# Output projection and first gate/up units of a two-layer decoder step: last squared sums moved ahead, one half-size product moved between two units, other PSUM banks for the last units

## The reference

```python
def rmsnorm(x, g):
    y = x * lax.rsqrt(jnp.mean(x * x, axis=-1, keepdims=True) + EPS)
    return y * g
...
# per layer
m = mixers(rmsnorm(x, g_pre_mix) @ w_in)          # one combined input projection
x = x + rmsnorm(m @ w_out, g_post_mix)            # output projection
h = rmsnorm(x, g_pre_ffn)
x = x + rmsnorm((silu(h @ w_gate) * (h @ w_up)) @ w_down, g_post_ffn)
...
# mixer C: scores of the token indexer
sc = relu(einsum('bthd,bsd->bths', qi, ki))       # 4 index heads
scores = einsum('bth,bths->bts', wi, sc)
```

## Time and profile before

| what | us |
|---|---|
| median of 3 runs | 3017.16 |
| lowest, highest | 3014.57, 3017.43 |
| profiled execution, its own time | 3017.33 |
| its span in the trace | 3015.2 |
| PE busy | 2916.3 (97%) |
| DVE busy | 1783.4 (59%) |
| ACT busy | 1371.4 (45%) |
| POOL busy | 1119.2 (37%) |

### The profile page before, as it was taken

One profiled execution on the slowest core, in us unless ns is written; L12 is line 12 of the kernel. 1 busy time (PEld: TensorE's weight loads), 2 busy tenths in 40 slices (PEclk: granted clock), 3 DMA queues, 4 the chain that ended last, 5 costly groups with the idle time before them and its releaser, 6 DMA issues. The chain is left out here.

```text
span 3015.2 us, 53292 instructions
## 1 busy us (share of the span) xinstructions
PE 2916.3 (97%) x20746; PEld 2541.2 (84%) x20746; DVE 1783.4 (59%) x3508; ACT 1371.4 (45%) x2618; POOL 1119.2 (37%) x846
## 2 busy tenths in 40 slices
PE   8999999999999999999999999998999999999998
PEld 6777756559999999999977777665699999999998
DVE  5579675546865455444555896754578554554551
ACT  4367525555543333444333765354645333334442
POOL 3003031215346656554700110313152555564442
PEclk9999999999999999999999999999999999999999
DMA  5120225553222222667621112356523222236763
GB/s 181 43 65 29 96 89 183 194 187 126 84 76 86 75 82 77 193 183 221 177 71 46 38 46 96 125 174 204 196 63 102 86 65 78 86 98 202 212 195 115
DMA packets 392242, 357.58 MB, mean 119 GB/s; under 512 B 33601, under 2 KB 354010, under 8 KB 391994
## 3 DMA queue, kind: packets, MB, share of 16 engines
q1 hardware_dynamic: 371514, 282.86, 30.9%
q0 software_dynamic: 20480, 71.32, 7.0%
HBM read 299.66 MB, written 54.44 MB: 117 GB/s over the span
## 5 line engine op out<-in xcount | busy, mean ns | idle before, releaser
L750 PE MATMUL ps<-w_in_slots,hT 128*128 128x256 f32 (+1 forms) x2048 | 446.8, 374 | 3.8 <-PEq L214 2.1
L750 PEld LDWEIGHTS ps<-w_in_slots,hT 128*128 128x128 f32 x2048 | 373.0, 192 | 59.1 <-issue 12.8
L2971 POOL TENSOR_TENSOR t_lo<-t_raw,t_hi 128x512 fp32r<-128x512 f32 x190 | 257.0, 1353 | 308.1 <-ACT t_hi L2766 219.0
L2443 PE MATMUL ps<-a_lo,wd_hi 128*128 128x352 f32 x1056 | 345.8, 327 | 5.8 <-DVE a_lo L3120 5.3
L2443 PE MATMUL ps<-a_hi,wd_hi 128*128 128x352 f32 x1056 | 340.5, 322 | 0.0
L2443 PE MATMUL ps<-a_hi,wd_lo 128*128 128x352 f32 x1056 | 340.1, 322 | 0.0
L2994 POOL TENSOR_TENSOR wd_lo<-wd_raw,wd_hi 128x1024 fp32r<-128x1024 f32 x96 | 212.2, 2217 | 210.1 <-ACT wd_hi L2814 209.9
L3086 DVE TENSOR_TENSOR t_raw<-w_pair,w_pair 128x512 f32<-128x512 f32 x120 | 130.6, 1088 | 268.0 <-PE ps L2547 268.0
L2547 PE MATMUL ps<-s_lo,t_hi 128*128 128x264 f32 x960 | 273.4, 285 | 0.0
L2547 PE MATMUL ps<-s_hi,t_lo 128*128 128x264 f32 x960 | 273.2, 285 | 0.0
L2547 PE MATMUL ps<-s_hi,t_hi 128*128 128x264 f32 x960 | 272.8, 284 | 0.0
(11 more groups left out here) (424 smaller groups left out, 7065.2 us busy)
## 6 DMA issues: line engine op xcount, KB each, us to landing
wd_raw<-in_w_down SPq DMA_DIRECT2D x192, 192.0 KB, 3.0
wd_raw<-in_w_down SPq DMA_DIRECT2D x96, 256.0 KB, 3.4
a_in<-apark SPq DMA_DIRECT2D x132, 176.0 KB, 3.9
w_pair<-in_w_gate SPq DMA_DIRECT2D x40, 512.0 KB, 5.2
w_pair<-in_w_up SPq DMA_DIRECT2D x40, 512.0 KB, 5.1
w_in_slots<-in_w_in SPq DMA_DIRECT2D x18, 1024.0 KB, 5.4
apark<-a SPq DMA_DIRECT2D x40, 264.0 KB, 2.1
apark<-t_up SPq DMA_DIRECT2D x40, 264.0 KB, 4.0
```

The lines of the kernel that those rows point to most:

```text
L750: ins = pe.matmul(ps[:m, bank[i], 0:w], hT[:, k, cols(n)], W[:, g % 2, k, 0:w], start=(k == 0), stop=(k == KC - 1))
L2443: ins = pe.matmul(bank(b), w, x, start=first and i == 0, stop=end and i == 2)
L2971: pool.tensor_tensor(t_lo[e][:, :, :], t_raw[e][:, :, :] if len(src) > 1 else src[0], t_hi[e][:, :, :].bitcast(F32), ALU.subtract).then_in ...
```

## The change

1. Input projection: the sample tile `PT` of group CV moves from the last place to between tiles 4 and 5; the chunks of index scores 2 and 3 change places (the 128-column one now comes ahead of the 512-column one). In layer 1 the first `rotate` is issued inside `new_x_left`, at k = 5.
2. Banks: units 7 to 11 use banks 2, 3, 7, 4, 5 where they used 0, 1, 7, 2, 3.
3. PE: `mix_sum_2(0)` one block of three matmuls earlier; `mix_sum_1(2)` behind unit 0 where it was behind unit 1; `mix_sum_2(2)` in the middle of unit 6 where it was behind it; `product(0, 0)` between units 7 and 8 where it was behind unit 11.
4. ACT: `root(2)` before `keep(1, 6)`; `keep(2, 7)` and the rounding of the second weights (`split_w(1)`) ahead of the last three roundings of third 1; the rounding for product (0, 0) behind `root(6)`.
5. POOL: the first rest of the output weights waits for DVE's first rest of the activations.
6. DVE, last third: `sum_comb("s5")` before the wait for POOL's last sum, `sum_weight(0)` behind it, `rest_of_weight(0)` behind `invert(6)`, all ahead of the h loop. `multiply_up(0)` and `(1)` stay behind the h loop.
7. SP: the first `w_pair` loads ahead of the last stores of `xpark`.

```diff
-    units = [... (IX, range(T0, TILES)), (CV, range(T1, TILES))) for n in tiles]
+    units = [... (IX, range(T0, TILES)), (CV, (3, 4, PT, 5, 6, 7))) for n in tiles]
+    chunks[2], chunks[3] = chunks[3], chunks[2]
...
                 for k in range(KC):
+                    if k == 5:
+                        rotate(0)
...
-    unit_bank = lambda n: n if n < 7 else (0, 1, 7, 2, 3)[n - 7]
+    unit_bank = lambda n: n if n < 7 else (2, 3, 7, 4, 5)[n - 7]
...
             for n, (j, th) in enumerate(seq):
+                if n == 8:
+                    product(0, 0)
...
                 for k in range(KC):
+                    if (n, k) == (6, 4):
+                        mix_sum_2(2)
...
-                if n == 1:
+                if n == 0:
                     mix_sum_1(2)
-                if n == 6:
-                    mix_sum_2(2)
             for q in range(NQ):
-                for pos in range(7):
+                for pos in range(0 if q else 1, 7):
...
             keep(1, 5)
+            root(2)
             keep(1, 6)
-            root(2)
...
-            split_h(1, 4, 5, 6, 7)
+            split_h(1, 4)
             keep(2, 7)
+            split_w(1)
+            split_h(1, 5, 6, 7)
...
             root(6)
+            round_weight(0)
             split_h(2, *range(KC))
...
             for k in range(KC):
                 if k:
                     pool.wait_ge(wo_hi_done, k)
+                else:
+                    pool.wait_ge(m_lo, 1)
...
                 if th == 2:
+                    sum_comb("s5")
                     dve.wait_ge(x_add, 3 * (KC - 1))
-                    sum_comb("s5")
+                    sum_weight(0)
                 invert(2 * th + 2)
+                if th == 2:
+                    rest_of_weight(0)
```

More of the change, by code:

```diff
@@ L600, in mix_in @@
     T0, T1 = 5, 3
-    units = [(g, n, 0) for g, tiles in ((IX, range(T0)), (CV, range(T1)), (IX, range(T0, TILES)), (CV, range(T1, TILES))) for n in tiles]
+    units = [(g, n, 0) for g, tiles in ((IX, range(T0)), (CV, range(T1)), (IX, range(T0, TILES)), (CV, (3, 4, PT, 5, 6, 7))) for n in tiles]
     for g in range(CQ, len(blocks)):
@@ L1394, in _ @@
                 g, n, th = units[i]
-                if i in rope_at:
+                if i in rope_at and not (l and i == 0):
                     rotate(i)
@@ L2488, in _ @@
                             pe.wait_ge(m_lo, KC * th + k + 1)
+                        if (th, d, k) == (1, 6, KC - 1):
+                            mix_sum_2(0)
                         if (th, d, k) == (2, 6, 3):
@@ L2741, in silu @@
                 act.activation(sg_first[:, j // 2, of(th)], bank(unit_bank(n)), ACT.Silu).then_inc(sg_done, 1)
[L2743 to L2751, removed]
             def round_comb(n):
@@ L2766, in round_weight @@
                 act.activation(t_hi[e][:, :, :], t_raw[e][:, :, :] if len(src) > 1 else src[0], ACT.Copy).then_inc(t_hi_done, 1)
+            root(5)
+            split_w(2)
+            silu(0)
+            silu(1)
+            split_w(3)
+            square_x(2, *range(KC))
+            root(6)
+            round_weight(0)
+            split_h(2, *range(KC))
             def keep_product(q, pos):
                 act.wait_ge(p_mm, 7 * q + pos + 1)
+                if (q, pos) == (0, 0):
+                    act.wait_ge(mm, len(seq))
                 if q:
@@ L2785, in _ @@
             round_comb("s1")
-            for m in range(3):
+            for m in range(1, 3):
                 round_weight(m)
@@ L3039, in sum_comb, with sum_weight, rest_of_weight @@
                 dve.tensor_tensor(comb_raw[n][:, :, :] if n in s_at else comb_raw[n], x, z, op).then_inc(comb_sum, 1)
+            def sum_weight(m):
+                e, src = m % NT, weight(m)
+                if len(src) == 1:
+                    return
+                dve.wait_ge(w2_in[m // 7 % 2], 32 * (m // 14 + 1))
+                if m >= NT:
+                    dve.wait_ge(p_mm, m - NT + 1)
+                dve.tensor_tensor(t_raw[e][:, :, :], *src).then_inc(t_sum, 1)
+            def rest_of_weight(m):
+                e, src = m % NT, weight(m)
+                dve.wait_ge(t_hi_done, m + 1)
+                dve.tensor_tensor(t_lo[e][:, :, :], t_raw[e][:, :, :] if len(src) > 1 else src[0], t_hi[e][:, :, :].bitcast(F32),
+                                  ALU.subtract).then_inc(t_lo_done, 1)
             dve.wait_ge(g_in, 64)
@@ L3135, in _ @@
             sum_comb("s1")
-            sum_weight(0)
             sum_weight(1)
@@ L3142, in _ @@
             rest_of_comb("s5")
-            rest_of_weight(0)
             dve.wait_ge(mm, 11)
```

53 lines of the change are left out of this document (19 added, 34 removed).

## The result

| | us |
|---|---|
| before, median of 4 runs | 3017.3 (3014.57 to 3020.82) |
| changed, median of 4 runs | 3040.34 (3038.2 to 3040.76) |
| ratio | 1.0077, interval 1.0065 to 1.009 |
| span of the profiled execution | 3015.2 before, 3038.2 after |

The change makes the kernel slower by 23.0 us. The forecast was 3034.7 us with a range of 3027 to 3040: the sign, the place and the main mechanism are as forecast, one step of the sum failed, the size is 5.6 us short, and the time lies just outside the range.

A forecast was written before the change was run, and what follows sets the result against it. PE, busy 97% of the span, bounds the kernel, so only its waits count. Output projection +22.6, index chunks -3.2, layer 1's first turn -1.4, POOL's wait -0.6: +17.4 on 3017.3 gives 3034.7 us, range 3027 to 3040.

The forecast's parts named there:

- Unit 7 waits for the multiply: Output projection: unit 7's new bank awaits DVE's first multiply behind the h loop; PE stands still about 10.4 us per layer.
- Rival 1: The wait at unit 7 costs nothing, since the multiply is done when PE arrives; 3009.5 us, chance 0.04.
- The half clock: Behind the wait at unit 7 PE runs at granted clock 0.50, losing 2.2 us per layer.
- Product (0, 0): Moved between units 7 and 8, it adds 3.0 us before unit 11's end; the stretch behind, bounded by DVE, gains nothing.
- rival 2: The 22.89 us stretch behind unit 11 shrinks by 5 us per layer; 3024.7 us, chance 0.13 in full or part.
- rival 4: Longer PE waits behind unit 11 lower the clock again, index changes only move waits; 3039 to 3045 us, chance 0.10.
- S' = 807.4: Forecast start of mix_sum_2(2) inside unit 6, layer 0: 2.0 us earlier than 809.41; bounds 805.6 and 807.9.
- it comes 2.4 to 3.2 us earlier: DVE's invert(5), which waited 2.97 us for ACT, comes that much earlier, and with it DVE's additions to x.
- the delay by the large sum: DVE's sum s5 beside POOL's last sums delays them by most of its 2.36 us length, before mix_sum_2(2).
- The index chunks: Input projection: PE's waits of 1.88 and 1.73 us for ACT's copies shrink; -1.6 us per layer, -3.2 in all.
- POOL's wait: Output projection's start: PE's 1.04 us wait for DVE's first rest goes, partly returning; -0.6 us for both layers.
- The rest of the program: Outside the output projection stage, from index chunks and layer 1's first turn: 4.6 us less.

The follow-up runs named there:

- e9_w1_only: Kernel before with only the second weights' rounding ahead of the middle third's last three roundings and mix_sum_1(2) behind unit 0; 0.9991, 3011.78 us.
- e4_banks_only: Kernel before with only the new banks of units 7 to 11; 1.0078, 3037.87 us.
- e1: Changed kernel with DVE's first two multiplies ahead of the last third's third reciprocal, not behind its h loop; 0.9993, 3011.54 us.
- e8: Kernel before with the input projection's changes, POOL's wait, and the second third's sum and root earlier; 0.9977, 3009.57 us.
- e7: Kernel before with only POOL's wait for DVE's first rest of the activations; 1.0000, 2988.40 us on a faster chip.
- e11: Changed kernel with product (0, 0) back behind unit 11, new banks kept; 1.0049, 3002.29 us on a faster chip.
- e12: Changed kernel with product (0, 0) ahead of unit 7 instead of unit 8; 1.0038, 3001.14 us on a faster chip.
- e5: Changed kernel with the early multiplies, and the second weights' rounding and mix_sum_1(2) back in their old places; 0.9993, 3015.09 us.
- e3: Changed kernel with the early multiplies and DVE's large sum s5 back behind the wait for POOL's last sums; 0.9985, 3011.03 us.
- e10: Kernel before with input projection changes, POOL's wait, earlier middle-third sum and root, early second weights, mix_sum_2(2) inside unit 6; 0.9966, 2978.87 us, faster chip.

## Why the prediction was right and wrong

**Unit 7 waits for the multiply: right.** The prediction said 12.7 us from S to the end of that multiply and 37.3 us from S to E (807.4 to 844.7). Measured are 12.9 (810.51 to 823.39, where unit 7 starts) and 37.46. The banks alone bring the wait and as much loss as the whole change, and moving the multiply removes both. Rival 1 priced a kernel without that wait at 3009.5 us; with the early multiplies it is 3011.5.

**The half clock: right.** 2.2 us were added. In the trace 5.11 us run at 0.50 (4.36 in the earlier trace rows), and the 24 matmuls of unit 7 take 6.3 us instead of 3.9: 2.4 lost. What the prediction didn't have is that the clock also falls behind the short wait inside unit 6 (0.63 in both layers); it went unpunished only because unit 7 had to wait anyway.

**Product (0, 0): right.** 3.0 us in front of E, and nothing gained behind it. The stretch behind E was 22.88 to 22.90 us in all kernels and both layers. PE is busy for 18.70 of the 22.88 us in the changed kernel, where 17.9 was reckoned; the stretch is no shorter for it, so rival 2 falls. The time lies in the range that rival 4 gave (3039 to 3045), but not for its reasons: the waits behind E are 4.2 us in five pieces and the clock stays at 1.00 there, and the index waits did shrink.

**S' = 807.4, the step that failed.** The prediction let S come 2.0 us earlier; from block 7 that is 63.54 us, and measured were 65.64 and 65.46. The step that failed is "it comes 2.4 to 3.2 us earlier", said of `invert(5)`: the reciprocal starts 45.20 us after block 7 in the changed kernel, 45.19 before. The prediction overlooked that POOL's second sum of squares and its subtraction, moved ahead with the weights, meet DVE's h loop of the middle third, whose scale and rest have two inputs: the loop becomes 2.9 us longer and loses what the earlier root would have brought.

The second half of the term, the delay by the large sum, was right: taken at 1.8 us (805.6 to 807.4), measured 1.94 (S 65.64 us after block 7 with it early, 63.70 with it behind POOL's sums). That the two engines hold each other up is read from rows that overlap; no run has the early root without the overlap. The same rule of the Trainium skill ("SBUF — State Buffer", section "Who interferes with whom") was weighed for the large sum only, where the runs bear it out (POOL's sums 4.04 us beside it, 2.11 apart), and not for the step before it.

The step mis-sized the term by 2.1 and 1.9 us, 4.0 in all. With it the forecast would have been 3038.7. The rest of the difference is three terms that partly cancel: S to E was 0.4 us longer in all than forecast, start to block 7 gained 1.5 us more (3.0 for 1.56), and the rest of the program gained 2.5 us less (2.1 for 4.6).

**The smaller terms.** The index chunks were to give 1.6 us a layer; their two waits fell from 3.61 to 1.98 us. Both are still for ACT's copies, and not for DVE as the prediction had it for the first. Layer 1's first turn no longer waits. The root was to give 0.48 and gave 0.59. POOL's wait was to give 0.6 in all; alone it measures nothing, and layer 0's larger gain in the profile (-2.4 us from start to block 7) is partly the clock, which was at 0.50 there before (683.47 to 687.50 us) and at 1.00 after (683.59 to 688.00). In two other kernels without that wait the stretch took 61.48 (layer 0 of `e9_w1_only`) and 62.93 us (layer 1 of `e4_banks_only`), so such a difference needs no edit.

**The rest of the program.** The two profiled executions leave 2.1 us less outside the stage where 4.6 was forecast. Taken as the span less both stretches from the start of the output projection to the second pair, the rest is 2666.1, 2668.0 and 2661.7 us in the three traces without the input projection's changes (before, `e4_banks_only`, `e9_w1_only`) and 2658.2 to 2664.0 in the seven with them (the changed kernel and `e1` to `e8`, without `e4` and `e7`). The kernel before took 3014 to 3017 us on the chips of all of them. The means differ by 4.0 us, with 6 us between the traces of one group, and the input projection's changes alone gave 4 us less. So the runs speak for the forecast of this term, and the 2.1 is what one pair happened to show; how the 4 us divide among the three edits stays open.

## What to carry to other kernels

- Changing a buffer number changes who releases it. Before moving a unit to another bank, find the instruction that frees the bank and read what stands ahead of it on its engine: here five bank numbers cost 23 us, because the reader stood behind an h loop of 8 us, and the clock fell behind the wait.
- A gap filled by moving work ahead is only a gain if the engine it is taken from is the bound in the place that it leaves; 3 us of PE work taken out of a stretch that DVE bounds came back as 3 us of delay for DVE's start.
- When an operation is moved on POOL, look at which two-input operations of DVE it will now meet, not only at whether its result is ready in time. Here 2.9 us gained on ACT were lost again on DVE.

## What the hardware did that was not expected

**Waits of 2 to 2.4 us mostly bring the clock down, at one and the same place not always.** Twelve stretches of these runs have a wait of 1.98 to 2.38 us inside unit 6. Behind ten of them the granted clock was 0.58 to 0.67 in the mean of the next 4.1 us: both layers of the changed kernel, of the kernel with the product back, and of `e11` and `e12`, and layer 1 of `e1` and `e5`. In layer 0 of `e1` and `e5` it stayed at 1.00. Behind the four waits of 0.43 to 0.46 us (`e3`, `e10`) it stayed at 1.00. In the kernel with the early multiplies the waits are 2.37 us in layer 0 and 2.36 in layer 1. The windows of 5 us from the end of each wait, layer 1 first (us, PE busy, clock, DMA share, GB/s):

```profile
2290.70:2295.70 5.00, 5.00 (x20) 0.66 0.21 72
808.56:813.56 5.00, 5.00 (x29) 1.00 0.21 72
```

In layer 1 a clock of 0.66 in the mean let 20 matmuls through, in layer 0 29. S to E is 26.19 us there and 24.81 here (26.27 and 24.70 in `e5`). So a wait that is free by its length can cost another 1.4 to 1.6 us. With the product back the same fall costs nothing: S to E is 24.48 us in both layers, since PE waits for DVE's rests in unit 8 in any case.

The attention stage shows the same between two executions. PE waits 2.76 us until 590.88 in the kernel before and 2.77 us until 590.42 in the changed one, in code that the change doesn't touch. The same window of each, before and then changed:

```profile
590.00:595.00 5.00, 3.78 (x25) 1.00 0.95 349
```

```profile
590.00:595.00 5.00, 4.58 (x16) 0.50 0.98 357
```

The executions of one kernel spread over some 3 to 16 us, and by and large the slower ones have the lower mean clock: of 25 executions of the kernel before the fastest took 3009.28 us at 0.994, the slowest 3021.25 at 0.990. A mean that is 0.004 lower is, as an estimate, 24 us more at 0.50, which costs 12 us, the whole difference. So a difference of 2 us between two traces can't be put down to an edit without the place where it arose.

**DVE's two-input scale is held up too.** Not only DVE's additions and subtractions: `SCALAR_TENSOR_TENSOR` took 2.70 us beside POOL's subtraction, 0.58 alone. The reciprocal, with one input, was not: 2.35 us from 789.53 in the kernel before, beside POOL's subtraction until 790.10 and the next one, and 2.35 from 812.00 in the changed kernel, where POOL was idle. The next subtraction, in the kernel before:

```profile
790.52 2.41 POOL L2940 TENSOR_TENSOR w_lo<-w_raw,w_hi 128x1024 fp32r<-128x1024 f32 x1 [0.42 <-ACT w_hi L2697]
```
